# Prompt attention scores as three fp32r passes of split q and k, and a weight split moved behind the attention

## The chip, the cores and the metric

The kernel runs on one core of one Trainium2 chip. The metric is the device time of one execution in microseconds. A core has five engines that run side by side and meet at semaphores: TensorE (PE), VectorE (DVE), ScalarE (ACT), GpSimd (POOL) and SyncE (SP, which here issues DMAs).

## What is computed

One layer of a hybrid decoder: for 1,024 prompt tokens and 32 sample tokens (8 sequences of 4), with 1,024 channels. Each row is normalised and projected by one combined matrix; one half of the result goes through causal window sums, the other through an attention of 8 heads of 64 channels in which an indexer picks 256 admissible keys for each query. Then come an output projection with a residual add and an MLP with squared ReLU. The part that the change touches:

```python
def attend(q, kg, vg, valid):
    logits = jnp.einsum('bqhd,bqkhd->bqhk', q.astype(jnp.float32), kg.astype(jnp.float32)) * (HEAD_DIM ** -0.5)
    logits = jnp.where(valid[:, :, None, :], logits, NEG_INF)
    p = jax.nn.softmax(logits, axis=-1)
    out = jnp.einsum('bqhk,bqkhd->bqhd', p, vg.astype(jnp.float32))
...
h = x + jnp.einsum('bte,ed->btd', jnp.concatenate([pool_out, attn_out], axis=-1), w_out)
```

The kernel doesn't gather keys. It computes the scores of all keys up to the query's block, adds a mask that is 0 for picked keys and -1e30 for the others, and takes the softmax over the row.

## The kernel before

The program is written by hand, one instruction list for each engine, with semaphores between them. Numbers that need fp32 accuracy in cheap matmuls are **split**: `hi` is the value rounded to fp32r, `lo` the rest, and a product is the sum of three fp32r passes (`hi*hi`, `hi*lo`, `lo*hi`; the helper `three`). That holds for the input projection, the output projection and the MLP. The attention's own products (`qk`, the transposes `p_T`, the values `pv`) are plain fp32.

The stages in order: norm and input projection, with the indexer and a search for each query's threshold beside it; four small fp32 products of the window sums (`pooled` by `wpool`); the **prompt attention**; then sample attention mixed with the first output-projection tiles; the rest of the output projection; MLP up and down; final norm.

The prompt attention has 8 blocks of 128 queries (j = 0 to 7) and in each 4 units (c = 0 to 3) of two heads. A unit's scores have 128(j+1) columns, cut into halves of up to 512 (`n_half`). For unit u, PE does in this order: `p_T(2u)` (transposes of the first head's probabilities, L2262), `qk(u+2, (0,))` (first half of the scores of the unit after next), `p_T(2u+1)`, `qk(u+2, (1,))` (the second half, blocks 4 to 7 only), for every second unit `spread_T` (L2288), and `pv(u)`. In `qk` the two heads of a unit sit in rows 0 to 63 and 64 to 127 of `qT` and `kT`, and write to two PSUM banks:

```python
mm(ps[:, 0:w], qT[r0:r0 + DH, c, P * j:P * j + P],
   kT[r0:r0 + DH, c, 512 * hf:512 * hf + w], True, True).then_inc(fullof(name), 1)
```

DVE adds the mask and finds the row maximum (L1755), ACT takes the exponential (L1209), PE transposes, ACT and DVE copy the transposes to `probT` (L1017, L1789), and PE multiplies by the values. Beside that DVE prepares the mask of block j+3 in parts: `flag` and `eq` (L1718, L1720), a scan over ties (L1723), a compare and multiply of two SBUF tiles (L1725). POOL spreads the denominators (`spread`, L852), finishes masks (`mask_sum`, L867 and L870) and makes the low part of the attention output (`o_low`, L860), two `q` steps for each block, in the order of `rows_half`.

POOL also splits the weights. `proj_split(n)` (L690, L692) takes block n of the weight columns in four quarters, high and low part of each; only the last quarter's low part raises `s_wlo`, for which PE waits before it uses the block. Block n lies in slot n % 2 of `w_raw`, `w_hi` and `w_lo`. Blocks 0 to 18 belong to `w_in`; block 19, `N_OUT`, is the first of `w_out`. Before, `N_OUT` is split ahead of the attention:

```python
for n in range(5, N_OUT + 1):
    proj_split(n)
```

and `N_OUT + 1` and the next follow behind the last `o_low`. After the attention PE runs `page_T(0)` (transposes of a page of the sample's cache), then `k_tile(0)`, the first output tile: three transposes of the residual (L2403), the wait for `s_wlo`, and 24 fp32r products. SP issues its loads in one order; the load of weight block `N_OUT + 2` (L524) waits until block `N_OUT` is split, and the cache pages of the next units (L558) stand behind it.

## Time and profile before

| | us |
|---|---|
| median of 3 runs | 1364.81 |
| lowest and highest | 1363.1, 1366.77 |
| the profiled execution, its own time | 1369.43 |
| its span, first to last instruction | 1367.6 |
| mean granted TensorE clock | 0.985 |

The span is cut by the order of stages: the attention runs from about 315.7 to 449 us, the first output tile's fp32r products begin at 452.2. All times in rows are microseconds from the span's start unless marked ns. A matmul row's length reaches past the start of the next row, since matmuls are pipelined; what a product occupies is read from start to start. An fp32 product stands in the trace as two records. "64*128 64x512" is a product with 64 rows and 128 stationary columns, and 512 moving columns.

### The profile page before, as it was taken

What the parts mean: (1) busy time and instruction counts of PE and PEld (TensorE: products, weight loads), DVE (VectorE), ACT (ScalarE), POOL (GpSimd) and SP (SyncE); (2) the same over time, 40 slices, a digit from 0 to 9 for tenths busy, and PEclk for the clock granted to TensorE, in tenths of its full rate; (3) what the DMA queues carried; (4) which work ended last, traced back from release to release, by engine and by line L of the source; (5) the groups of instructions that cost most, each with busy time, mean ns of one, the idle gap of its engine ahead of it and who ended that gap; (6) DMA issues with size and microseconds to landing.
All of it is one profiled execution on the core that took longest, in us unless ns stands there. A gap on an engine that the chain in (4) does not pass through costs nothing.

```text
span 1367.6 us, 25243 instructions
## 1 busy us (share of the span) xinstructions
PE 1320.3 (97%) x9720; PEld 1222.1 (89%) x9720; DVE 696.3 (51%) x1611; ACT 533.6 (39%) x1075; POOL 583.8 (43%) x607
## 2 busy tenths in 40 slices
PE   5999999999999999999899999999899999999998
PEld 4958999995666899779899999999899999999997
DVE  6368996767985222237834434434534334333445
ACT  6344887737777222325433333333301110111034
POOL 5333984342330311321277667677233333333610
PEclk9999999998999999999999999999999999999999
DMA  6330113310000876772233323323521331232203
GB/s 196 84 90 16 47 55 95 94 48 1 1 25 25 280 230 197 250 237 93 79 110 126 106 84 126 110 79 126 190 94 63 110 110 64 92 110 103 68 2 127
DMA packets 143549, 141.68 MB, mean 104 GB/s; under 512 B 21080, under 2 KB 111320, under 8 KB 143423
## 3 DMA queue, kind: packets, MB, share of 16 engines
q1 hardware_dynamic: 124933, 116.31, 26.7%
q10 hardware_dynamic: 17842, 21.94, 4.4%
q0 software_dynamic: 656, 1.84, 0.6%
q8 instruction: 77, 1.26, 0.4%
q14 instruction: 41, 0.34, 0.1%
HBM read 111.87 MB, written 26.50 MB: 101 GB/s over the span
## 4 chain that ended last, share of the span: by engine, by line
PE 80%; DVE 7%; ACT 3%; issue 1%; POOL 0%; ACTq 0%; DVEq 0%; POOLq 0%
PE bank L2087 73%; PE bank L2262 3%; DVE junk L1664 3%; PE bank L2324 2%; ACT sjunk L1119 1%; DVE lack L1668 1%; PE bank L2403 1%; PE bank L2132 0%; PE bank L2591 0%; DVE cc_lo L1743 0%; DVE cand L1674 0%; DVE hid_lo L2012 0%; DVE sqacc L1875 0%; PE bank L2288 0%; DVE delta L1671 0%
## 5 line engine op out<-in xcount | busy, mean ns | idle before, releaser
L2087 PE MATMUL bank<-hid_hi,w_hi 128*128 128x384 f32 (+1 forms) x672 | 219.6, 327 | 3.9 <-DVE stg L1937 3.9
L2087 PE MATMUL bank<-hid_hi,w_lo 128*128 128x384 f32 (+1 forms) x672 | 218.0, 324 | 0.0
L2087 PE MATMUL bank<-hid_lo,w_hi 128*128 128x384 f32 (+1 forms) x672 | 215.4, 323 | 0.0
L2044 DVE TENSOR_TENSOR acc<-bank,acc 128x384 f32<-128x384 f32 x168 | 87.7, 524 | 206.6 <-PE bank L2087 206.6
L690 POOL TENSOR_TENSOR w_hi<-w_raw,zero 128x256 fp32r<-128x256 f32 x108 | 68.6, 635 | 207.1 <-PE bank L2087 190.6
L2087 PE MATMUL bank<-xn_hi,w_hi 128*128 128x384 f32 (+1 forms) x456 | 151.5, 332 | 2.0 <-POOL w_lo L692 1.3
L904 POOL TENSOR_TENSOR w_hi<-w_raw,zero 128x1024 fp32r<-128x1024 f32 x29 | 54.9, 1893 | 223.4 <-PE bank L2087 205.4
L2087 PE MATMUL bank<-xn_lo,w_hi 128*128 128x384 f32 (+1 forms) x456 | 148.1, 325 | 0.0
L2087 PE MATMUL bank<-xn_hi,w_lo 128*128 128x384 f32 (+1 forms) x456 | 147.6, 324 | 0.0
L1411 ACT ACTIVATE hid_hi<-hraw 128x1056 fp32r<-128x1056 f32 x32 | 32.7, 1077 | 258.2 <-PE bank L2087 167.2
L2087 PEld LDWEIGHTS bank<-hid_hi,w_hi 128*128 128x128 f32 x672 | 127.8, 190 | 4.2 <-DVE stg L1937 4.2
L2087 PEld LDWEIGHTS bank<-hid_hi,w_lo 128*128 128x128 f32 x672 | 127.6, 190 | 0.0
L2087 PE MATMUL bank<-hi_T,hn_hi 128*128 128x264 f32 x448 | 127.5, 285 | 0.0
L2087 PE MATMUL bank<-lo_T,hn_hi 128*128 128x264 f32 x448 | 127.0, 283 | 0.0
L2087 PE MATMUL bank<-hi_T,hn_lo 128*128 128x264 f32 x448 | 126.8, 283 | 0.0
L2087 PEld LDWEIGHTS bank<-hid_lo,w_hi 128*128 128x128 f32 x672 | 125.9, 188 | 0.0
L1119 ACT ACTIVATE sjunk<-score,cand 128x768 bf16<-128x768 f32 (+2 forms) x93 | 96.6, 1041 | 22.4 <-DVE cand L1674 18.0
L1664 DVE TENSOR_SCALAR_CACHE_REDUCE junk<-score,cand 128x384 uint8<-128x384 f32 (+1 forms) x124 | 101.7, 876 | 3.7
L2087 PE MATMUL bank<-hn_hi,hn_lo 128*128 128x264 f32 x336 | 95.7, 285 | 0.0
L2087 PE MATMUL bank<-hn_hi 128*128 128x264 f32 x336 | 95.5, 284 | 0.0
L2087 PE MATMUL bank<-hn_lo,hn_hi 128*128 128x264 f32 x336 | 95.2, 283 | 0.0
L908 POOL TENSOR_TENSOR w_lo<-w_raw,w_hi 128x1024 fp32r<-128x1024 f32 x32 | 77.2, 2414 | 38.0 <-ACT w_hi L1397 26.7
(300 smaller groups left out, 3227.2 us busy)
## 6 DMA issues: line engine op xcount, KB each, us to landing
w_raw<-in_w_ff_dram SPq DMA_DIRECT2D x50, 512.0 KB, 3.5
hraw<-hidden_dram SPq DMA_DIRECT2D x16, 1056.0 KB, 7.4
page<-in_cache_k_dram SPq DMA_DIRECT2D x64, 256.0 KB, 3.7
page<-in_cache_v_dram SPq DMA_DIRECT2D x64, 256.0 KB, 3.5
hidden_dram<-stg ACTq DMA_DIRECT2D x56, 264.0 KB, 2.0
w_raw<-in_w_in_dram SPq DMA_DIRECT2D x18, 512.0 KB, 3.6
wr<-in_w_ff_dram SPq DMA_DIRECT2D x14, 512.0 KB, 4.5
xrow<-in_x_prompt_dram SPq DMA_DIRECT2D x8, 512.0 KB, 8.1
```

What stands on the lines that cost most here:

```text
L690: nc.gpsimd.tensor_tensor(w_hi[n % 2][:, c], w_raw[n % 2][:, c], zero_w[:, 0:WP], ALU.add).then_inc(s_whi, 1)
L904: nc.gpsimd.tensor_tensor(w_hi[n[0] % 2][:, :], w_raw[n[0] % 2][:, :], zero_w, ALU.add).then_inc(s_whi, 1)
L908: nc.gpsimd.tensor_tensor(w_lo[n[0] % 2][:, :], w_raw[n[0] % 2][:, :], w_hi[n[0] % 2][:, :].bitcast(F), ALU.subtract).then_inc(s_wlo, 1)
L1119: nc.scalar.activation(sjunk[i % 2][0:r, 0:n], v, ACT.Sign, bias=cand[0:r, ND + i:ND + i + 1].bitcast(F), scale=-1.0, accum_out=cnt[0:r, N ...
L1411: nc.scalar.activation(hid_hi[slot][:, k, :], src[:, k, :], ACT.Copy).then_inc(s_hh, 1)
L1664: nc.vector.tensor_scalar(junk[0:r, i % 2, 0:n], v, cand[0:r, i:i + 1].bitcast(F), 0.0, ALU.is_lt, ALU.add, accum_out=cnt[0:r, i:i + 1]).t ...
L1668: nc.vector.tensor_tensor(lack[:, :], cnt[:, :], lim[:, :], ALU.is_gt).then_inc(s_bs, 1)
L2044: nc.vector.tensor_tensor(v, ps[:, 0:w], v, ALU.add).then_inc(freeof(("dn", gi, m, g)), 1)
L2087: return nc.tensor.matmul(out, lhsT, rhs, start=start, stop=stop)
L2262: last = nc.tensor.transpose(ps[:, P * (k - 4 * hf):P * (k - 4 * hf) + P], prob[:, i % 4, P * k:P * k + P], ident[:, :])
L2324: last = nc.tensor.transpose(ps[:, P * c:P * c + P], page[i % PS][:, j, P * c:P * c + P], ident[:, :])
L2403: nc.tensor.matmul(ps[:, P * (t - a):P * (t - a) + P], xblk[xi][:, t, :], ident[:, :], start=t == a, stop=False, is_transpose=True)
```

## The change

Four new tiles hold the split operands. `q_hi` and `q_lo` lie in the halves of the norm buffers that the attention output fills later, `k_lo` lies on `kT` itself, and `k_hi` lies on `w_hi` and `w_lo` of both slots. So no weight block can be split while the attention still reads `k_hi`: block `N_OUT` leaves the loop ahead of the attention and is split behind the last `o_low`, after a wait for the last scores. POOL splits q and k of blocks 0 and 1 before the attention and of block j+2 in the `spread` step of block j (`qk_split`, 4 instructions of 128x512, 8 calls). PE makes three passes for each pair of halves, both heads in turn within each pass, and waits for `s_qk` at the first unit of each block.

```diff
+        q_hi = at("q_hi", A_X + C4 * T * 4, [P, C4, T], R)
+        q_lo = at("q_lo", A_X + XN + C4 * T * 4, [P, C4, T], R)
+        k_hi = at("k_hi", A_W + 2 * KC * P * 4, [P, C4, NP], R)
+        k_lo = at("k_lo", A_K, [P, C4, T], R)
...
-            for n in range(5, N_OUT + 1):
+            for n in range(5, N_OUT):
                 proj_split(n)
...
+            def qk_split(j):
+
+                cols = slice(P * j, P * j + P)
+                zero_t = zero[:, 0:1].unsqueeze(2).broadcast_to([P, C4, P])
+                nc.gpsimd.tensor_tensor(k_hi[:, :, cols], kT[:, :, cols], zero_t, ALU.add).then_inc(s_qk, 1)
+                pool.wait_ge(s_qk, 4 * j + 1)
+                nc.gpsimd.tensor_tensor(k_lo[:, :, cols], kT[:, :, cols], k_hi[:, :, cols].bitcast(F), ALU.subtract).then_inc(s_qk, 1)
+                nc.gpsimd.tensor_tensor(q_hi[:, :, cols], qT[:, :, cols], zero_t, ALU.add).then_inc(s_qk, 1)
+                pool.wait_ge(s_qk, 4 * j + 3)
+                nc.gpsimd.tensor_tensor(q_lo[:, :, cols], qT[:, :, cols], q_hi[:, :, cols].bitcast(F), ALU.subtract).then_inc(s_qk, 1)
+
+            for c in range(C4):
+                for g in range(3):
+                    wait_evac(pool, ("proj", N_Q + c, g))
+            qk_split(0)
+            qk_split(1)
...
+                    if q % 2 == 0 and q // 2 + 2 < QB:
+                        qk_split(q // 2 + 2)
...
             o_low(2 * QB - 1)
-            for n in range(N_OUT + 1, N_OUT + KM + 2):
+            for u in (NU - 2, NU - 1):
+                for e in range(2):
+                    for hf in range(n_half(units[u][0])):
+                        wait_full(pool, ("qk", 2 * u + e, hf))
+            for n in range(N_OUT, N_OUT + KM + 2):
                 proj_split(n)
...
             def qk(u, halves=(0, 1)):
...
+                if c == 0 and halves[0] == 0:
+                    pe.wait_ge(s_qk, 4 * j + 4)
...
-                    for e in range(2):
-                        r0 = DH * e
-                        name = ("qk", 2 * u + e, hf)
-                        ps = begin(pe, name)
-                        mm(ps[:, 0:w], qT[r0:r0 + DH, c, P * j:P * j + P],
-                           kT[r0:r0 + DH, c, 512 * hf:512 * hf + w], True, True).then_inc(fullof(name), 1)
+                    for i, (a, b_) in enumerate(((q_hi, k_hi), (q_hi, k_lo), (q_lo, k_hi))):
+                        for e in range(2):
+                            r = slice(DH * e, DH * e + DH)
+                            name = ("qk", 2 * u + e, hf)
+                            ps = bank[plan[name][0]] if i else begin(pe, name)
+                            last = mm(ps[:, 0:w], a[r, c, P * j:P * j + P], b_[r, c, 512 * hf:512 * hf + w], i == 0, i == 2)
+                            if i == 2:
+                                last.then_inc(fullof(name), 1)
```

On POOL ahead of the attention, the instructions between the last `w_in` block and the first `spread`; before:

```order
L690 TENSOR_TENSOR w_hi_138<-w_raw_136,zero 128x256 [waits bank5_full,weights_loaded1]
L692 TENSOR_TENSOR w_lo_140<-w_raw_136,w_hi_138 128x256 [waits weights_high]
...
L852 COPY rdenb<-rden 128x256 [waits denominator] x2
L867 TENSOR_TENSOR cum<-cum,flag 128x512 [waits mask_ties_ranked]
L870 TENSOR_SCALAR score<-cum 128x512 [waits mask_summed]
```

and with the change:

```order
L866 TENSOR_TENSOR k_hi<-kT,zero 128x4x128 [waits bank3_free,bank4_free,bank2_free,bank5_free,bank1_free,bank0_free]
L868 TENSOR_TENSOR k_lo<-kT,k_hi 128x4x128 [waits attention_operands_split]
L869 TENSOR_TENSOR q_hi<-qT,zero 128x4x128
L871 TENSOR_TENSOR q_lo<-qT,q_hi 128x4x128 [waits attention_operands_split]
...
L859 COPY rdenb<-rden 128x256 [waits denominator]
L866 TENSOR_TENSOR k_hi<-kT,zero 128x4x128
L868 TENSOR_TENSOR k_lo<-kT,k_hi 128x4x128 [waits attention_operands_split]
L869 TENSOR_TENSOR q_hi<-qT,zero 128x4x128
L871 TENSOR_TENSOR q_lo<-qT,q_hi 128x4x128 [waits attention_operands_split]
L859 COPY rdenb<-rden 128x256 [waits denominator]
```

The eight instructions of weight block `N_OUT` are gone from here; blocks 0 and 1 of k and q stand in their place, and block 2 stands between the first and the second `spread`.

On POOL behind the attention, before:

```order
L860 TENSOR_TENSOR cc_lo<-onorm,cc_hi 128x2x128 [waits attention_high]
L852 COPY rdenb<-rden 128x256 [waits bank7_full,denominator]
L860 TENSOR_TENSOR cc_lo<-onorm,cc_hi 128x2x128 [waits attention_high] x2
L690 TENSOR_TENSOR w_hi_137<-w_raw_135,zero 128x256 [waits bank2_full,weights_loaded0]
L692 TENSOR_TENSOR w_lo_139<-w_raw_135,w_hi_137 128x256 [waits weights_high]
```

and with the change:

```order
L884 TENSOR_TENSOR cc_lo<-onorm,cc_hi 128x2x128 [waits attention_high]
L859 COPY rdenb<-rden 128x256 [waits bank7_full,denominator]
L884 TENSOR_TENSOR cc_lo<-onorm,cc_hi 128x2x128 [waits attention_high] x2
L697 TENSOR_TENSOR w_hi_142<-w_raw_140,zero 128x256 [waits bank2_full,bank1_full,bank0_full,bank3_full,weights_loaded1,bank5_full]
L699 TENSOR_TENSOR w_lo_144<-w_raw_140,w_hi_142 128x256 [waits weights_high]
```

The first split behind the last `o_low` was that of slot 0 (block `N_OUT + 1`) and is now that of slot 1 (block `N_OUT`), with slot 0 behind it. On PE the reader of that block has not moved:

```order
L2437 MATMUL bank<-ident,xblk_68 128x128 [waits x_block0,bank6_free,attention_low]
L2437 MATMUL bank<-ident,xblk_68 128x128 x2
L2117 MATMUL bank<-cc_hi,w_hi_142 128x384 [waits weights_low]
L2117 MATMUL bank<-cc_lo,w_hi_142 128x384
L2117 MATMUL bank<-cc_hi,w_lo_144 128x384
```

It is still the first output tile, directly behind the three residual transposes, and `w_hi_142` is slot 1.

## Rows read from the trace of the kernel before

**Rows 1.** The page: engines over the span, then the chain by engine.

```profile
PE 1320.3 (97%) x9720; PEld 1222.1 (89%) x9720; DVE 696.3 (51%) x1611; ACT 533.6 (39%) x1075; POOL 583.8 (43%) x607
...
PE 80%; DVE 7%; ACT 3%; issue 1%; POOL 0%; ACTq 0%; DVEq 0%; POOLq 0%
```

**Rows 2.** Stretches of the attention: length, busy time of each engine, PEclk, DMA.

```profile
316.00:334.40 18.40, 16.73 (x86) 9.20 (x83) 13.57 (x63) 11.39 (x45) 4.28 (x7) 0.63 0.00 1
334.40:361.00 26.60, 26.60 (x226) 16.64 (x224) 25.16 (x80) 22.24 (x64) 9.12 (x13) 1.00 0.01 2
361.00:376.70 15.70, 15.02 (x123) 9.42 (x123) 14.10 (x48) 11.24 (x27) 5.04 (x6) 1.00 0.01 2
376.70:400.70 24.00, 23.64 (x211) 15.36 (x211) 20.66 (x66) 16.48 (x40) 7.93 (x15) 1.00 0.01 2
400.70:436.50 35.80, 35.80 (x317) 23.00 (x316) 22.20 (x76) 25.39 (x50) 6.73 (x9) 1.00 0.11 30
```

**Rows 3.** Chain of waits between 361 and 376.7 us, shares of that stretch.

```profile
by line: PE bank L2087 24.2%; DVE prob L1755 20.7%; DVE cum L1723 11.9%; issue 11.4%; PE bank L2262 9.6%; DVE flag L1718 8.1%; DVE nmx L1774 4.6%; DVE eq L1720 3.1%; DVE probT L1789 2.5%; DVE rden L1797 1.1%; DVE need L1722 0.9%; DVE mx L17
```

**Rows 4.** Timeline of PE in block 6: start, length, engine, line, operation, operands.

```profile
403.99 1.13 PE L2087 MATMUL bank<-kT,qT 64*128 64x512 f32 x4
405.05 0.98 PE L2262 MATMUL bank<-ident,prob 128*128 128x128 f32 x7
405.96 0.92 PE L2087 MATMUL bank<-kT,qT 64*128 64x384 f32 x4
```

**Rows 5.** PE's timeline, score products of 128 columns.

```profile
366.21 0.49 PE L2087 MATMUL bank<-kT,qT 64*128 64x128 f32 x4
366.63 0.44 PE L2288 MATMUL bank<-ident,rdenb 128*128 128x128 f32 x2
```

**Rows 6.** PE's timeline, fp32 products over 128 rows, 4,224 columns in all.

```profile
308.49 7.26 PE L2087 MATMUL bank<-pooled,wpool 128*128 128x384 f32 x24
```

**Rows 7.** The chain in order of time: fp32r products, 288 and 384 columns.

```profile
207.49 3.20 PE bank L2087 x24
210.79 4.21 PE bank L2087 x24
```

**Rows 8.** Timeline of DVE, one scan; of DVE and POOL, sums beside a split.

```profile
373.67 2.71 DVE L1723 TENSOR_TENSOR_SCAN cum<-eq 128x1024 f32<-128x1024 bf16 x1
...
602.69 1.22 DVE L1875 TENSOR_TENSOR sqacc<-sqacc,sqt 128x384 f32<-128x384 f32 x2 [5.76 <-ACT sqt L1309]
606.36 1.89 POOL L904 TENSOR_TENSOR w_hi<-w_raw,zero 128x1024 fp32r<-128x1024 f32 x1 [12.03 <-PE bank L2087]
607.00 4.08 DVE L1875 TENSOR_TENSOR sqacc<-sqacc,sqt 128x256 f32<-128x256 f32 x2 [3.09 <-ACT sqt L1309]
```

**Rows 9.** One line on POOL: minimum/median/maximum ns, first and last start.

```profile
L933 POOL TENSOR_TENSOR hn_lo<-w_raw,hn_hi x49: 1289/1297/1310, 683.7 to 941.3; 128x512 fp32r<-128x512 f32 x49
```

**Rows 10.** Timeline of ACT and POOL at the attention's start.

```profile
308.69 0.41 ACT L1017 ACTIVATE qT<-bank 128x288 f32<-128x288 f32 x1 [2.71 <-PE bank L2087]
...
321.56 0.40 POOL L852 COPY rdenb<-rden 128x256 f32<-128x256 f32 x1 [17.81 <-DVE rden L1797]
```

**Rows 11.** Timeline of POOL after the attention, first and last of eight.

```profile
451.69 0.61 POOL L690 TENSOR_TENSOR w_hi<-w_raw,zero 128x256 fp32r<-128x256 f32 x1
...
456.52 0.73 POOL L692 TENSOR_TENSOR w_lo<-w_raw,w_hi 128x256 fp32r<-128x256 f32 x1
```

**Rows 12.** PE's timeline, first product that reads w_out.

```profile
452.20 0.42 PE L2087 MATMUL bank<-cc_hi,w_hi 128*128 128x384 f32 x1
```

**Rows 13.** PE's timeline, an earlier wait for a split.

```profile
662.17 0.69 PE L2087 MATMUL bank<-hn_hi,w_hi 128*128 128x384 f32 x1 [5.53 <-POOL w_lo L908]
```

**Rows 14.** Stretches after two waits of PE, columns as in rows 2.

```profile
662.20:665.40 3.20, 3.20 (x10) 3.20 (x11) 3.20 (x2) 1.16 (x2) 2.71 (x1) 0.50 0.13 46
...
976.90:982.90 6.00, 6.00 (x20) 6.00 (x21) 0.23 (x1) 4.25 (x5) 2.10 (x1) 0.50 0.97 367
```

**Rows 15.** Timeline of SP's issues after the attention.

```profile
452.86 0.42 SPq L524 DMA_DIRECT2D w_raw<-in_w_out_dram  x1
```

More of the change, by code:

```diff
@@ L195, in hymba_pool_dsa_step @@
         assert C4 * NB * HQ + G * SK <= moff[QB] and C4 * NB * HQ + G * (SK + (NPG + 1) * P) <= moff[QB] + T
+        q_hi = at("q_hi", A_X + C4 * T * 4, [P, C4, T], R)
+        q_lo = at("q_lo", A_X + XN + C4 * T * 4, [P, C4, T], R)
+        k_hi = at("k_hi", A_W + 2 * KC * P * 4, [P, C4, NP], R)
+        k_lo = at("k_lo", A_K, [P, C4, T], R)
+        assert C4 * NP <= 4 * KC * P
         acc = at("acc", A_Q, [P, KC, T], F)
@@ L460, in hymba_pool_dsa_step @@
         s_rd = sem("denominator")
+        s_qk = sem("attention_operands_split")
         s_exp_on = sem("exponential_loaded")
```

## The prediction

> **What bounds the kernel now.** I read the page first: PE is busy for 97% of the span and makes up 80% of the chain that ended last [rows 1], so a change counts by what it does to PE's path. The second view cuts the attention into stretches [rows 2]. PE is busy nearly throughout, but so is DVE in some: 25.2 of 26.6 us from 334.4 to 361, 14.1 of 15.7 up to 376.7, 20.7 of 24 up to 400.7. Only from 400.7 on has DVE much room (22.2 of 35.8). In the first stretch the granted clock is 0.63 on average, so most of it ran at 1.2 GHz and not 2.4. The third view, the chain between 361 and 376.7 us, gives PE's matmul line only 24% and DVE's lines over half [rows 3]: there a faster score product doesn't help. Then the timeline of PE shows what a score product occupies, and the timelines around 452 us show who needs the moved weight block.
>
> **What the score products cost.** A pair of halves (two heads) starts at 403.99 and PE's next work at 405.05: 1.06 us for 512 columns [rows 4]. For 128 columns it is 366.21 to 366.63, 0.42 us [rows 5]. A line through both gives 1.67 ns a column and 0.21 us fixed; so 0.85 for 384 and 0.63 for 256 columns. Full-height fp32 products, 4,224 columns in 7.26 us, take 1.72 ns a column for one product [rows 6]. A pair costs as much as one, so the two heads run side by side in their row halves.
>
> An fp32r pass takes 3.20/24 = 0.133 us for 288 columns and 4.21/24 = 0.175 for 384 [rows 7], a line that gives 0.232 for 512, 0.119 for 256 and 0.063 for 128. No row shows an fp32r pair in row halves. If it runs side by side as the fp32 pairs do, a pair costs 0.21 plus three passes: 0.90, 0.73, 0.57 and 0.40 us for 512, 384, 256 and 128 columns. If it doesn't, it costs 0.21 plus six: 1.60, 1.26, 0.92 and 0.59. I take the first, since the nearest rows (same operand places, same banks) show it. There are 24 pairs of 512 columns and 8 of each other width. **Gross gain:** 24 x 0.16 + 8 x (0.12 + 0.06 + 0.02) = 5.4 us; at the lower clock the four pairs of block 1 save about twice as much, 0.3 more: 5.7. The other end is a loss of 24 x 0.54 + 8 x (0.41 + 0.29 + 0.17) = 19.9.
>
> A rule speaks of the same quantity. The Trainium skill's page FP8 and Floating Point Precision (section Matmul Precision) says that true fp32 is four passes through the array; by its count three in place of four would take a quarter off. Of the 40.6 us that all pairs take that is 10.2, and the sum below would end 4.8 us lower. The rows disagree in size: a pass of fp32r has 0.45 ns a column against 0.42 in fp32, and the fixed 0.21 us isn't divided.
>
> **How much of 5.7 reaches the end.** By stretch [rows 2]: up to 334.4 blocks 0 and 1 can save 0.6, and I take 0.5. Up to 361 blocks 2 and 3 can save 1.1, but DVE has 1.4 us of room, which the next part eats; 0.3. Up to 376.7 nothing [rows 3]. Up to 400.7 about 1.2, of which 0.8; up to 436.5 about 2.1, of which 1.5, because the second half's product also covers the copies of the transposed probabilities, and in every second unit nothing else stands between. That makes 3.1.
>
> **The new POOL work.** A subtraction of 128x512 on POOL takes 1.30 us [rows 9]; the add with zero is bounded by 0.61 (half as wide) [rows 11] and that 1.30, and I take 1.1. One `qk_split` is 2 x (1.1 + 1.3) = 4.8 us (3.8 to 5.2). The last q columns leave ACT at 309.1, so block 0 is split by 313.9; PE ends the window products at 315.7 [rows 6, 10], so `qk(0)` doesn't wait. Block 1 is done by 318.7, ahead of the first `spread` at 321.56 [rows 10]. That cover is 1.8 us; if it fails, PE waits for the rest. The later splits stand in POOL's queue before an `o_low` and the next `spread`, half a block (4 us and more) later; I cost the queue at nothing. Where POOL is late, the second `spread` of block 0 is the first to show it.
>
> But POOL's instruction holds up DVE's with two SBUF operands. Two sums of 384 columns took 1.22 us together; two of 256 beside a weight split took 4.08 [rows 8]. The six later splits fall on DVE's scans (2.71 us the largest) and some of its multiplies [rows 8], with a delay between nothing and one POOL instruction each: 0 to 1.3 us, six to nine times. Up to 361 this is in my 0.3; for the rest I take 0.6 off. **Net gain of the attention: 2.5 us**, with ends at 5.7 and at -1. The Trainium skill says the same of the cause (GPSIMD Engine Reference, Specifications: the SBUF interfaces are shared with VectorE, contention with two SBUF inputs), and the trace agrees. By that rule every scan beside a split would wait, which would put the gain nearer 1.
>
> **The moved weight split.** Ahead of the attention its removal gives nothing: POOL idles 17.8 us there anyway [rows 10]. Behind it, POOL's first split of a block runs from 451.69 to 457.25, eight instructions [rows 11], and there is now block `N_OUT`. PE reads it at 452.20 [rows 12] and gets `s_wlo` only at the end: **5.1 us** of wait, with nothing else for PE since its queue is in order. The last `o_low`, which starts the split, ends with the attention, so this wait doesn't shrink when the attention does. Block `N_OUT+1` is then done at 462.8, long before the fourth output tile. SP holds the load at 452.86 [rows 15] and the pages behind it until 457.3, 4.4 us; PE itself is 5.1 later, so I cost that at nothing.
>
> Such a wait also costs clock. A wait of 5.53 us for a split [rows 13] was followed by work at 0.50 until 665.4, 3.2 us; after another wait, of 3.9 us, 6.0 us of work ran at 0.50 [rows 14]. Half of it is lost: 1.6 to 3.0 us. I take **2.3**.
>
> **Sum:** -2.5 + 5.1 + 2.3 = +4.9 us on the profiled execution's 1369.4, so 1374.3. That execution lies 4.6 us above the median of 1364.8; for the median I say **1369.7**. A measurement of this kernel can tell about 0.3%, 4.1 us, from no change.
>
> **Rivals.**
> *The gain arrives whole.* PE's savings are not eaten by DVE: -5.7 + 5.1 + 1.6 to 3.0 gives +1 to +2.4, near 1366.5. For it: PE leads the chain in four of five stretches. Against: DVE at 95% between 334 and 361. By the page's count of passes it would be -2.8, 1362. Together 0.27.
> *The clock returns earlier in the attention* (faster). From 316 to 334.4 the mean is 0.63, about 13.6 us at half speed [rows 2], worth up to 6.8 us of PE time. The change alters how PE is loaded there. If all of it went and the gain came whole: 1.7 - 6.8 = -5.1, 1359.7. It decides when over 5.8 of the 6.8 come back; DVE, 13.6 of 18.4 busy, makes that unlikely. Chance 0.05.
> *More half-speed work or DVE in the lead.* A further 3.4 us at 0.50 within the attention costs 1.7, and all scans held up bring the gain to 0: +9, 1373.9. Chance 0.12.
> *The fp32r pair isn't side by side*: +19.9 + 7.4 = +27, 1392. Against it, only the fp32 rows. Chance 0.04.
> *The change doesn't do what it says* would be `qk(0)` held by a late split; past its 1.8 us of cover each us costs one. That is inside the range.
>
> **How the numbers follow.** The forecast has 0.52, the others 0.27, 0.05, 0.12 and 0.04. Of the forecast's share about 0.4 lies above +4.1, with the two slower rivals 0.56 to 0.6; the 0.27 and the rest of the forecast are no measurable change. So faster 0.05, same 0.37, slower 0.58. The range takes in the first and third rivals: 1364.5 to 1374.5.
>
> **What would show it.** Right: the pairs' start-to-start falls to about 0.90 and 0.73 us; an idle of about 5 us before the first fp32r product of `w_out`, released by POOL, then some us at clock 0.50; scans longer than before beside the new splits; the attention 2 to 3 us shorter. Wrong: pairs of 1.6 us; no idle at that place; or an attention shorter by 5 us or more.

## The result, and the profile after

The changed kernel took 1374.88 us (median of 4 runs, 1374.75 to 1375.19), the kernel before 1364.70 (4 runs, 1363.1 to 1366.77). The ratio is 1.0074, with a 95% interval of 1.0057 to 1.0091: slower by 10.2 us, where +4.9 was forecast and 1374.5 was the upper end of the range. The profiled execution took 1374.97 us with a span of 1373.2. Against the profiled execution of before (1369.43, span 1367.6) that is +5.5, which is nearly the forecast. The two comparisons don't agree, since the profiled execution of before lies above all four of those runs; the section on the reasons comes back to that.

The page after, engines and chain (compare [rows 1]):

```profile
PE 1317.8 (96%) x9816; PEld 1231.7 (90%) x9816; DVE 698.4 (51%) x1611; ACT 533.7 (39%) x1075; POOL 630.5 (46%) x639
...
PE 76%; DVE 9%; ACT 3%; issue 2%; POOL 1%; DVEq 0%; ACTq 0%; POOLq 0%
```

POOL has 32 more instructions and 46.7 us more of work; PE is busy for 2.5 us less. PE's share of the chain fell by 4 points, and DVE, issue and POOL took them.

PE's timeline in block 6 (compare [rows 4]):

```profile
405.03 0.50 PE L2117 MATMUL bank<-k_hi,q_hi 64*128 64x512 f32 x2
405.37 0.40 PE L2117 MATMUL bank<-k_lo,q_hi 64*128 64x512 f32 x2
405.60 0.39 PE L2117 MATMUL bank<-k_hi,q_lo 64*128 64x512 f32 x2
405.92 0.98 PE L2296 MATMUL bank<-ident,prob 128*128 128x128 f32 x7
406.84 0.45 PE L2117 MATMUL bank<-k_hi,q_hi 64*128 64x384 f32 x2
407.12 0.34 PE L2117 MATMUL bank<-k_lo,q_hi 64*128 64x384 f32 x2
407.30 0.34 PE L2117 MATMUL bank<-k_hi,q_lo 64*128 64x384 f32 x2
407.57 0.44 PE L2322 MATMUL bank<-ident,rdenb 128*128 128x128 f32 x2
```

A pair of 512 columns takes 0.89 us from its start to the next work (405.03 to 405.92), one of 384 takes 0.73. Each row holds the two instructions of one pass, one for each head. The three rows of a pair start 0.34 and 0.23 us apart, where one product of 512 columns over all rows would take 0.23 by the line through [rows 7], and six of them 1.39. So the fp32r products of two heads do run side by side in their row halves.

The stretches of the attention (compare [rows 2]):

```profile
334.40:361.00 26.60, 25.39 (x242) 18.14 (x240) 24.99 (x70) 22.31 (x64) 23.74 (x21) 0.99 0.01 2
361.00:376.70 15.70, 14.36 (x134) 10.19 (x136) 14.16 (x52) 10.03 (x26) 10.30 (x11) 1.00 0.01 2
376.70:400.70 24.00, 22.38 (x230) 16.57 (x228) 20.89 (x67) 17.42 (x40) 18.34 (x22) 1.00 0.00 1
400.70:436.50 35.80, 35.51 (x361) 26.77 (x361) 23.83 (x79) 26.04 (x53) 6.98 (x9) 1.00 0.10 31
```

Where POOL went from 9 to 24 us (first row) and from 8 to 18 (third), PE's busy time fell by 1.2 and 1.3 us, and PE stands idle instead. Between 355 and 366 us the chain of waits changes its leader. The first line is from before, the second from after:

```profile
by line: PE bank L2087 68.7%; PE bank L2262 29.3%; PE bank L2288 3.3%
```

```profile
by line: DVE prob L1785 37.3%; issue 30.7%; DVE cum L1755 12.0%; DVE flag L1748 8.4%; DVE eq L1750 5.5%; PE bank L2117 4.5%; DVE cum L1753 3.4%; DVE nmx L1804 2.5%; DVE nmx L1807 1.7%; DVE rden L1827 1.6%; DVE mx L1785 1.1%; DVE onorm L1836
```

The timelines of POOL and DVE there show what happened:

```profile
356.14 0.40 POOL L859 COPY rdenb<-rden 128x256 f32<-128x256 f32 x1 [1.21 <-DVE rden L1827]
356.50 1.04 POOL L866 TENSOR_TENSOR k_hi<-kT,zero 128x512 fp32r<-128x512 f32 x1
357.62 1.28 POOL L868 TENSOR_TENSOR k_lo<-kT,k_hi 128x512 fp32r<-128x512 f32 x1
358.85 2.76 POOL L869 TENSOR_TENSOR q_hi<-qT,zero 128x512 fp32r<-128x512 f32 x1
361.69 1.28 POOL L871 TENSOR_TENSOR q_lo<-qT,q_hi 128x512 fp32r<-128x512 f32 x1
```

```profile
357.68 3.10 DVE L1753 TENSOR_TENSOR_SCAN cum<-eq 128x896 f32<-128x896 bf16 x1
```

In before the same scan, of 896 columns, took 2.01 us:

```profile
357.45 2.01 DVE L1723 TENSOR_TENSOR_SCAN cum<-eq 128x896 f32<-128x896 bf16 x1
```

The scan comes to its turn 0.06 us after `k_lo` started, stands until 358.85, and then takes its 2.0. `q_hi` stands until the scan is through and takes the rest of its own 1.0 after that. The later of the two stands until the earlier is through: DVE is 1.1 us later, POOL 1.7. The Trainium skill has this as a rule (SBUF — State Buffer, section "SBUF: two separate sides": an exclusive lock, whichever starts first has it for the whole instruction), and the trace agrees.

POOL paid this at every split beside the attention: the two splits ahead of it take 4.74 us each, the six others 5.9 to 6.8, of which the four from 343 us on 6.5 to 6.8. DVE paid at some: of the six scans, three are longer than in before (two by 0.5 to 0.6 us, one by 1.1) and three are not. One of those three had stood behind POOL already in before, where an `o_low` was under way when it came to its turn:

```profile
373.51 0.73 POOL L860 TENSOR_TENSOR cc_lo<-onorm,cc_hi 128x256 fp32r<-128x256 f32 x1 [1.61 <-ACT cc_hi L1225]
```

So the 2.71 us of [rows 8] hold a wait. In the kernel with high parts by copy (below) the scan of 1,024 columns met almost none:

```profile
373.02 2.29 DVE L1755 TENSOR_TENSOR_SCAN cum<-eq 128x1024 f32<-128x1024 bf16 x1
```

POOL's queue was the second thing. Half a block earlier a split had made the next `spread` late, and PE waited for it:

```profile
351.20 0.39 POOL L859 COPY rdenb<-rden 128x256 f32<-128x256 f32 x1
```

```profile
351.64 0.44 PE L2322 MATMUL bank<-ident,rdenb 128*128 128x128 f32 x2 [0.86 <-POOL rdenb L859]
```

Its input `rden` was ready at 349.51, while the split was still running. In [rows 10] the first `spread` had followed its `rden` at once.

Last, the moved weight split: the wait of PE, and the stretches of the wait, of the work at half clock behind it, and of the work after (compare [rows 12, 14]):

```profile
456.57 0.69 PE L2117 MATMUL bank<-cc_hi,w_hi 128*128 128x384 f32 x1 [4.83 <-POOL w_lo L699]
```

```profile
451.76:456.57 4.81, 0.00 (x0) 0.00 (x0) 0.39 (x1) 0.00 (x0) 4.58 (x8) 0.76 0.44 122
456.57:461.14 4.57, 4.57 (x14) 4.57 (x15) 0.00 (x0) 0.00 (x0) 4.33 (x7) 0.50 0.76 257
461.14:470.00 8.86, 8.86 (x84) 8.33 (x84) 1.38 (x2) 1.63 (x3) 0.83 (x2) 1.00 1.00 323
```

PE stands for 4.8 us, the granted clock falls within that wait, and PE then works at 1.2 GHz for 4.57 us, of which half is lost: 2.3.

### The profile page after: what moved, and what is told of

It is laid out like the page before. It is cut to its first block, busy times and chain, and to the rows that moved or that the text cites. A ratio compares the mean times of both kernels' runs of the same rounds, so it can differ in the third digit from the quotient of the medians.

```text
span 1373.2 us, 25484 instructions
## 1 busy us (share of the span) xinstructions
PE 1317.8 (96%) x9816; PEld 1231.7 (90%) x9816; DVE 698.4 (51%) x1611; ACT 533.7 (39%) x1075; POOL 630.5 (46%) x639
## 4 chain that ended last, share of the span: by engine, by line
PE 76%; DVE 9%; ACT 3%; issue 2%; POOL 1%; DVEq 0%; ACTq 0%; POOLq 0%
PE bank L2117 70%; DVE junk L1694 3%; PE bank L2358 2%; PE bank L2296 2%; ACT sjunk L1149 1%; DVE prob L1785 1%; DVE lack L1698 1%; PE bank L2437 1%; PE bank L2162 0%; PE bank L2625 0%; DVE cc_lo L1773 0%; DVE cand L1704 0%; DVE hid_lo L2042 0%; DVE sqacc L1905 0%; DVE delta L1701 0%
```

## The experiments

Two measures need explaining. The first: the attention has 16 reciprocals `rden`, one for each half block q, and they mark its course. The time from the sixth to the last (q=5 to q=15) lies behind the half-clock work of the attention's start and ahead of the wait for the weight block, so it compares the attention's inside at full clock, in all kernels but the one with the splits at odd q. In before it was 97.12 us in both profiles of that kernel, and in after 96.93 and 96.84 in its two.

The second runs from the last of these reciprocals to the next one, in the sample attention, and holds the wait for the weight block with the clock behind it. From 446.96 to 553.66 in before it is 106.70 us, in after 113.83 and in its second profile 113.99:

```profile
446.96 0.17 DVE L1797 RECIPROCAL rden<-den 128x4 f32<-128x4 f32 x1
553.66 0.15 DVE L1856 RECIPROCAL rden<-den 128x1 f32<-128x1 f32 x1
```

```profile
446.27 0.17 DVE L1827 RECIPROCAL rden<-den 128x4 f32<-128x4 f32 x1
560.10 0.15 DVE L1886 RECIPROCAL rden<-den 128x1 f32<-128x1 f32 x1
```

So the moved split costs 7.1 to 7.3 us there.

**The kernel before, profiled again.** No edit.

> The kernel before, unchanged, profiled once more. Its runs spread from 1363.1 to 1366.8 us and its profiled execution took 1369.4, while those of the changed kernel lie within 0.5 us and its profiled execution among them. Theory: executions of the kernel before differ by stretches of work at a granted clock of 0.50 after waits of PE (each costs about 1.7 us per 3.4 us of stretch), and the profiled one had more of them than the median one. Then a new profile near 1365 shows less half-clock time than the first one, by about 2 x 4.5 = 9 us in all. Rival: the profiled execution was longer in idle time (transfers, semaphores) at the same clock; then the half-clock stretches are the same and idle gaps of PE are longer.

It came out at 1365.73 us (10 runs, 1360.71 to 1369.78), ratio to the kernel before 0.9995 (0.998 to 1.0011). The profiled run was again the longest: 1369.78 at a mean granted clock of 0.985, with the same stretches at half clock as in the first profile, but for one of 3.4 us that lies at 28 us and not at 106. So the place of the difference within an execution was not seen. What was seen is the list of runs. Over these 10 and the 68 runs of before that stand beside the experiments, the fastest took 1360.5 us at a mean clock of 0.995 and the slowest 1371.7 at 0.984, and on the whole the mean time falls as the clock rises (1367.8 at 0.987, 1366.3 at 0.989, 1363.7 at 0.993). (1 - clock) times the span is 6.8 us in the fastest and 21.9 in the slowest, 15 apart where the times are 11 apart. The list supports the theory. Since both profiles are of long executions, it doesn't rule out that waits differ as well.

**The move alone.** The kernel before with

```
-            for n in range(5, N_OUT + 1):
+            for n in range(5, N_OUT):
...
-            for n in range(N_OUT + 1, N_OUT + KM + 2):
+            for n in range(N_OUT, N_OUT + KM + 2):
```

> The kernel before with only the weight split of block N_OUT moved behind the last o_low; scores stay fp32, no splits of q and k. Theory A (the loss is the moved split): PE waits about 5 us before its first w_out product of block N_OUT and then works some 7 us at half clock, so +6.5 us or more (4.4 to 5.1 of wait, 2.3 of clock), +8 to +10 if a later stretch of half clock comes on top, since the changed kernel is 10.2 above the median. Theory B (the loss sits in the new work of POOL inside the attention): +4 us or less here.

1372.26 us against 1365.90, ratio 1.0052 (1.0033 to 1.0071): +6.4. PE's wait is the same 4.83 us as in after, and the work behind it runs at half clock. q=5 to q=15 took 96.89 us, and from the last reciprocal to the next 113.52, 6.8 more than in before. Theory A gets its lower number. The move is about two thirds of the loss, and not the 8 to 10 us which would have made it all.

**Splits that nobody reads.** The changed kernel, its score products replaced by those of before:

```
-                    for i, (a, b_) in enumerate(((q_hi, k_hi), (q_hi, k_lo), (q_lo, k_hi))):
...
+                    for e in range(2):
...
+                        mm(ps[:, 0:w], qT[r0:r0 + DH, c, P * j:P * j + P],
+                           kT[r0:r0 + DH, c, 512 * hf:512 * hf + w], True, True).then_inc(fullof(name), 1)
```

> The changed kernel with all its splits of q and k on POOL and PE's wait for them, but the score products are the fp32 ones of the kernel before (the parts are made and not read; the low part of k goes to the place of the low part of q, so that k stays whole). Against the kernel with the move alone it prices POOL's new work. Theory A (queue and port cost little): 0 to 1 us above the move alone. Theory B (POOL's splits hold DVE's scans and the spreads, and eat the gain of the products): 2 to 5 us above the move alone. Against the changed kernel it prices the products: 5 to 6 us above it if the products gain their whole worth, 1 to 2 if DVE and POOL hide them anyway.

1376.68 us, 4.4 above the move alone (ratio to before 1.0086, 1.0064 to 1.0107). q=5 to q=15 took 99.08, 2.2 more than with the move alone. The scan of 896 columns took 3.08 us here too:

```profile
358.02 3.08 DVE L1753 TENSOR_TENSOR_SCAN cum<-eq 128x896 f32<-128x896 bf16 x1
```

So POOL's new work costs 2.2 us in that part, and 4.4 in the whole of a run. Of the rest the profiles show 0.7 from q=0 to q=5 (27.99 against 27.29) and 1.0 from the last reciprocal to the next (114.49 against 113.52), but there the stretches at half clock differ too. Against the kernel that does use the splits, the products gain 2.2 us from q=5 to q=15 (99.08 to 96.9). The medians give 2.2 as well (1376.7 to 1374.5 of the repeat below), but the runs of the two kernels overlap. Theory B holds in size for the splits, theory A's "5 to 6 us" for the products doesn't.

**The weight split in a gap.** In POOL's program, after:

```
-            rows_half(QB + 2, 2 * QB)
-            o_low(2 * QB - 1)
+            rows_half(QB + 2, 2 * QB - 1)
...
-            for n in range(N_OUT, N_OUT + KM + 2):
+            proj_split(N_OUT)
+            rows_half(2 * QB - 1, 2 * QB)
+            o_low(2 * QB - 1)
+            for n in range(N_OUT + 1, N_OUT + KM + 2):
```

> The changed kernel, but the weight split of block N_OUT runs on POOL between the o_low of q=13 and the spread of q=15, as soon as the last scores are read, and not behind the last o_low. Theory A (the loss of the change is that wait with its clock): the wait before the first w_out product goes, and the time falls by 5 us of wait and 2 to 5 of clock: 1365 to 1368. What is left against the kernel before is then the net of products and POOL work, about -0.7 by the attention's end in the traces. Theory B: the split delays the last spread and o_low instead, and the gain is under 3 us.

1367.53 us, ratio to before 1.0018 (1.0005 to 1.003). POOL's timeline, first and last of the split, then the last spread:

```profile
437.49 0.61 POOL L697 TENSOR_TENSOR w_hi<-w_raw,zero 128x256 fp32r<-128x256 f32 x1
...
442.32 0.73 POOL L699 TENSOR_TENSOR w_lo<-w_raw,w_hi 128x256 fp32r<-128x256 f32 x1
445.47 0.40 POOL L859 COPY rdenb<-rden 128x256 f32<-128x256 f32 x1 [2.42 <-DVE rden L1829]
```

The split ends 2.4 us ahead of the next `spread`, and PE goes into the first `w_out` product without a wait and at full clock. From the last reciprocal to the next it is 106.70 us, as in before. 7 us of the loss were the place of that one block, and this place was allowed: the last scores are read by then, so nobody needs `k_hi` any more. 1.6 us are left. q=5 to q=15 takes 96.95, as in before, and the mean clock of the runs was 0.988 against 0.9895; what the 1.6 us are made of isn't shown.

**The splits at odd q.** On top of the kernel with the split in the gap:

```
-                    if q % 2 == 0 and q // 2 + 2 < QB:
-                        qk_split(q // 2 + 2)
                     if q >= 1:
                         o_low(q - 1)
+                    if q == 0:
+                        qk_split(2)
+                    if q % 2 == 1 and q // 2 + 3 < QB:
+                        qk_split(q // 2 + 3)
```

> The kernel with the split of block N_OUT in the gap, and the splits of q and k moved in POOL's order: block 2 behind o_low at q=0, blocks 3 to 7 behind o_low at odd q, where DVE runs no scan; before, they stood behind the spread at even q, beside the scans. In the traces so far the half blocks from q=5 to q=15 take 96.89 us with the move alone, 99.08 with the unused splits and 96.95 with splits and products; 1.97 of those 2.2 us come in q=6 and q=7, where a scan went from 2.01 to 3.08 us and a spread waited behind a split. Theory B (splits beside scans and before the spread are the price): scans return to 2.01 and 2.71 us, q=5 to q=15 falls to about 95 us, and the time to 1365.5. Rival C (POOL's work itself is the price, wherever it stands): the spread or o_low that now waits is another one, and q=5 to q=15 stays at 97.

A miss of 7 us: 1372.65, ratio to before 1.0058 (1.0036 to 1.008). At odd q POOL has its mask sums to do and the next `spread` comes soon. Two of the splits met a scan there too (at 332 and 359 us) and took 5.9 and 6.7 us; the three others at odd q took 4.8 to 5.0. The next `spread` stood behind the whole split:

```profile
359.28 2.86 POOL L871 TENSOR_TENSOR q_lo<-qT,q_hi 128x512 fp32r<-128x512 f32 x1
362.09 0.39 POOL L859 COPY rdenb<-rden 128x256 f32<-128x256 f32 x1
```

```profile
362.54 0.33 PE L2326 MATMUL bank<-ident,rdenb 128*128 128x128 f32 x1 [3.09 <-POOL rdenb L859]
```

Two such waits, 3.29 us at 335.8 and 3.09 at 362.5, both followed by half clock, stand against the 5 us lost to the kernel with the split in the gap. q=5 to q=15 took 99.08, but here this part holds one of the waits and the half clock behind it (3.4 us from 363.2). Without these 3.1 and 1.7 us it would be some 94.3, an estimate, as short as with no later splits at all (below). Theory B was half of the matter: the scan of that block took 2.32 us in place of 3.09, where it had said 2.01, and the queue cost more than the lock had.

**High parts by copy.** On top of the split in the gap, for `k_hi`, and for `q_hi` alike:

```
-  nc.gpsimd.tensor_tensor(k_hi[:, :, cols], kT[:, :, cols], zero_t, ALU.add)
+  nc.gpsimd.tensor_copy(k_hi[:, :, cols], kT[:, :, cols])
```

> The kernel with the split of block N_OUT in the gap, and the high parts of q and k made by POOL's copy (one operand) in place of the add with zero. Theory (only an instruction with two operands in SBUF shuts DVE's out, and the other way round): a q_hi beside the scan takes its undisturbed time in place of 2.2 to 3.0 us, the low parts still hold DVE, the copy takes 0.6 to 1.04 us, and q=5 to q=15 falls by 0.5 to 1 us, the time to 1366.5 to 1367. Rival: a copy is held by DVE like the add, and nothing changes.

1365.82 us, ratio to before 0.9998 (0.9983 to 1.0014). q=5 to q=15 falls to 94.76.

```profile
355.10 0.62 POOL L866 CAST k_hi<-kT 128x512 fp32r<-128x512 f32 x1
355.80 1.28 POOL L868 TENSOR_TENSOR k_lo<-kT,k_hi 128x512 fp32r<-128x512 f32 x1
357.02 2.35 POOL L869 CAST q_hi<-qT 128x512 fp32r<-128x512 f32 x1
359.45 1.28 POOL L871 TENSOR_TENSOR q_lo<-qT,q_hi 128x512 fp32r<-128x512 f32 x1
```

A copy alone takes 0.62 us where the add with zero took 1.04, so a split is 0.84 us shorter. But the copy beside the scan took 2.35: it waited for the scan as the add had. The reason given in the expectation is wrong, since with one operand too POOL waited for the scan, and the gain from q=5 to q=15 is 2.2 us where 0.5 to 1 was expected. POOL's instructions are the whole edit, so they are the cause: a split beside the attention takes 5.0 to 5.9 us in place of 5.9 to 6.8. Which of the waits behind them went first wasn't taken apart.

**The wait filled.** The changed kernel, in PE's first `w_out` tile, before its wait for the low parts:

```
+                    if m == 0 and g == 0:
+                        fill = begin(pe, ("proj", n, 1))
+                        for _i in range(28):
+                            mm(fill[:, 0:384], cc_hi[:, C4, 0:P], cc_hi[:, C4, 0:384], True, True)
                     pe.wait_ge(s_wlo, n + 1)
```

> The changed kernel, with PE's wait of 4.8 us before the first w_out product filled by 28 fp32r products of 384 columns into the bank of the next tile, which that tile's first transposes overwrite; nothing else is altered and no result is. 28 x 0.16 = 4.5 us and a start-up, so the wait nearly goes from idle to busy and the first real product starts when it did, at most 0.5 us later. Theory (the idle costs clock on top of its own length): no stretch of granted clock 0.50 follows at 454 us, and the time is 2 to 3 us below the changed kernel. Rival (the half-clock stretch comes from something else, or costs nothing because other engines lead there): the stretch or the time stays, 0 to 0.5 us.

1371.45 us (7 runs, 1370.28 to 1373.07) against 1374.5 for the changed kernel again (below). The first stretch is the filled wait, the second the work behind it:

```profile
451.00:456.00 5.00, 5.00 (x29) 4.68 (x29) 0.21 (x1) 0.00 (x0) 4.76 (x8) 1.00 0.39 114
456.00:461.10 5.10, 5.10 (x34) 5.06 (x33) 0.01 (x1) 0.88 (x2) 4.79 (x8) 1.00 0.87 271
```

The first real product starts 5.65 us after POOL's first split instruction, 5.58 in after, so the wait is as long as it was; only PE was busy in it. The clock stays at 1.00. From the last reciprocal to the next it is 111.84 us: 5.1 more than in before, which is the wait, and 2.0 to 2.2 less than in the two profiles of after, which is the clock's share, with nothing else changed. The medians are 3.05 us apart, with runs that overlap; what they show above those 2.0 to 2.2 isn't placed.

**The changed kernel again.** No edit.

> The changed kernel once more, unchanged, for comparison with the variants on the same chip. Its first four runs lay within 0.5 us at 1375, at a granted clock of 0.985; runs of the kernel before spread over 9 us, from 1360.7 at 0.995 to 1369.8 at 0.985. Theory (executions differ only by how many half-clock stretches they draw, 3.4 us each and 1.7 us of loss): over more runs the changed kernel spreads too, its median falls below 1375 and the difference to the kernel before shrinks towards 8 us. Rival: it always pays all of its stretches, and stays at 1375.

1374.5 us (6 runs, 1371.96 to 1376.6) against 1365.47, ratio 1.0072 (1.0049 to 1.0094). It does spread, so its first four runs were close together by chance. But its median hardly falls, and the difference is 9 to 10 us, not 8. Its mean clock was 0.986. The profiled run had 0.991 and a span of 1370.2, 3.0 less than the first profile: the stretches of half clock at 106 and 201 us are absent from it, and the one at the attention's start is 3.4 us in place of 13.7. The wait of 4.82 us and the half clock behind it are there as in the first.

The two profiles show one thing more. From q=0 to q=5 they took 28.00 and 27.99 us, each step between two reciprocals the same to 0.01 us, though 13.7 us ran at half clock in the one and 3.4 in the other. So at the attention's start half clock cost the changed kernel nothing, since something other than PE's products set the pace. The fp32 kernels took 28.52 us there with 13.7 us at half clock (both profiles of before) and 27.29 with 8.6 (the move alone).

**The products alone.** On top of the split in the gap: no splits of q and k for blocks 2 to 7, whose products read other data of the same shape.

```
-                    if q % 2 == 0 and q // 2 + 2 < QB:
-                        qk_split(q // 2 + 2)
...
+                    ops = ((q_hi, k_hi), (q_hi, k_lo), (q_lo, k_hi)) if j < 2 else ((cc_hi, cc_hi),) * 3
```

> The kernel with the split of block N_OUT in the gap, without the splits of q and k for blocks 2 to 7: PE makes the same number of fp32r products of the same shapes there, on other data (the attention of these blocks is not the reference's). It gives the products' gain with none of POOL's work beside it. The half blocks from q=5 to q=15 took 96.89 us with fp32 products and no splits, 99.08 with splits alone, 96.95 with both. Theory B: POOL's later splits cost 2.2 us there whatever the products are, so 94.7 us here and about 1365.0 in time. Rival (the products' gain is itself hidden behind DVE, and the splits cost only where PE isn't ahead): 95.5 to 96.5 us, and the time stays within 1 us of the kernel with the splits.

q=5 to q=15 took 94.17 us: 2.7 less than with fp32 products, 2.8 less than with the splits beside them. The median is 1363.97, ratio to before 0.9992 (0.9981 to 1.0003): even without the later splits the products don't make the whole clearly faster. Theory B again. In that part of the attention the table of four is complete:

| q=5 to q=15 | no later splits | with them |
|---|---|---|
| fp32 products | 96.89 | 99.08 |
| three passes | 94.17 | 96.95 |

**Three blocks ahead.** High parts by copy, both copies ahead of both subtractions, `qk_split(0)` to `(2)` ahead of the attention and `qk_split(q // 2 + 3)` at even q.

> The kernel with high parts by copy, with three blocks split ahead of the attention in place of two (blocks 3 to 7 at q=0, 2, 4, 6, 8) and both copies ahead of both subtractions. A split takes 3.8 us now, so three end near 320.6, where the first spread is due at 320.4. Theory: one split fewer beside DVE's scans and the first subtraction later than the scan's start; q=0 to q=15 took 123.7 us and falls by 1 to 2, the time to 1364 to 1365. Rival: a subtraction that waits for a scan still ends late and holds the spread behind it, as with the splits at odd q, where PE waited 3.3 and 3.1 us for a spread; then it is no faster or slower by 1 to 3.

1364.33 us, ratio to before 0.9994 (0.9985 to 1.0003). q=0 to q=15 is 122.8 us, 0.9 less than with two blocks ahead (123.7). The direction is the theory's, but against the kernel before it can't be told from no change.

**All copies, and their control.** The last kernel with the high parts of POOL's weight splits made by `tensor_copy` as well, and the kernel before with that edit alone (three lines of the form `nc.gpsimd.tensor_copy(w_hi[n % 2][:, c], w_raw[n % 2][:, c])`).

> As the kernel with three blocks split ahead, and the high parts of all weight blocks that POOL splits made by its copy too (0.61 in place of 1.04 us for 512 columns). The weight splits also stand before waits of PE: 5.5 to 5.9 us at 652 to 664 and 3.9 at 970 to 980. Theory (these waits are POOL's two passes over a block, and the first pass is 2.1 of some 4.8 us): each wait shortens by 1 to 2 us, the time falls by 2 to 4 below the kernel with three blocks ahead, 1360 to 1362, faster than the kernel before. Rival: the transfer of the block or ACT's part leads there, and nothing changes.

> The kernel before with the same edit of the weight splits alone, as the control: if it falls as much as the theory gives the kernel with all copies (2 to 4 us, to 1362 or 1363), that gain has nothing to do with the scores, and the difference between the two is what the fp32r scores are worth after all: 1 to 2 us by the attention's length so far (123.7 against 125.6). Rival: no change, 1365.5.

1359.39 us, ratio 0.9954 (0.9939 to 0.9969), and 1359.65, ratio 0.9959 (0.9944 to 0.9974). Both beat both kernels, and they can't be told apart: the gain is that of the copies, and the fp32r scores add nothing that the whole shows. From q=5 to q=15 they are 2.3 us shorter (94.66 against 96.95), but the mean clock of these runs was 0.989 and that of the control 0.992; whether that takes the 2.3 us back isn't shown. The gain didn't come from where the theory had it. The waits at 650 and 965 us are still 5.8 and 3.9. What has gone is a wait of 1.9 us ahead of the attention, with the half-clock work behind it. In before, PE's timeline and the stretches:

```profile
200.67 0.63 PE L2132 MATMUL bank<-ident,vchunk 128*128 128x128 f32 x4 [1.92 <-ACT vrow L1017]
```

```profile
198.75:200.67 1.92, 0.00 (x1) 0.03 (x1) 1.89 (x5) 1.92 (x7) 1.84 (x4) 1.00 0.00 0
200.67:204.70 4.03, 4.03 (x16) 4.03 (x17) 3.84 (x8) 2.52 (x5) 3.87 (x5) 0.58 0.48 130
```

In the control PE has no wait there, and the clock stays at 1.00:

```profile
196.00:206.00 10.00, 10.00 (x68) 9.90 (x67) 7.72 (x16) 8.07 (x15) 7.34 (x9) 1.00 0.20 54
```

That wait ended with ACT, whose copies out of PSUM stand between its steps of the search for each query's threshold. DVE's part of that search has an addition of 7 columns that reads two SBUF tiles, once in each of 31 steps. Before, then the control (minimum, median and maximum in ns):

```profile
L1674 DVE TENSOR_TENSOR cand<-cand,delta x31: 166/167/2373, 126.2 to 286.4; 128x7 int32<-128x7 int32 x31
```

```profile
L1674 DVE TENSOR_TENSOR cand<-cand,delta x31: 165/167/583, 124.2 to 280.9; 128x7 int32<-128x7 int32 x31
```

Its longest wait beside POOL's splits went from 2.4 to 0.6 us, and the 31 steps take 3.5 us less. That speaks for POOL's shorter instructions holding DVE less. It accounts for 3.5 us of the 6; how much of the rest is the missing wait's clock and how much differs between executions anyway wasn't taken apart.

## Why the prediction was right and wrong

**The price of a pair** was right to 0.01 us: 0.90 and 0.73 forecast, 0.89 and 0.73 measured. A pair of 512 columns became 16% shorter. That the halves run side by side was a choice from the fp32 rows, and it held.

**The gain of the products** was right too. From 361 us on the forecast had 0, 0.8 and 1.5 in its last three stretches, 2.3 together; the experiment without the later splits gives 2.7 from q=5 (350 us) on.

**"The later splits stand in POOL's queue ... I cost the queue at nothing", and "for the rest I take 0.6 off"**: this is the step that failed within the attention. The splits cost 2.2 us (fp32 products) to 2.8 (three passes) from q=5 to q=15, not 0.6. Two things were missed. The lock works both ways: I let POOL hold DVE, by up to one instruction, and didn't let DVE's scan hold POOL, which made a 4.7 us split one of 5.9 to 6.8. And "half a block (4 us and more) later" isn't enough room for 6.5 us when an `o_low`, a `spread` and two mask sums want the same queue. Net, the attention became 0.7 us shorter between the two profiles (POOL's first weight split 451.69 before [rows 11], 450.99 after) where I had 2.5. The sentence that the rule of the shared interfaces "would put the gain nearer 1" was the better number, but by luck: it let every scan wait for POOL, and in the trace three of six became longer while POOL waited at all six.

**The moved split** was right: 5.1 us of wait forecast, 4.83 measured; 2.3 us of clock forecast, 2.3 read off the trace, and 2.0 to 2.2 gained by filling the wait. The pieces on the profiled executions make -0.7 + 4.8 + 2.3 = +6.4, and 0.5 more has come by 785 us, of which 0.3 lies in a wait of 5.85 us in place of 5.53 [rows 13]. Of that, the half clock behind the wait at 980 us gives back 1.5: 3.0 us of work in after, 6.0 in before [rows 14]. Measured +5.5, forecast +4.9. That the two are so near is in part luck: the attention gave 1.8 us less than forecast, and the shorter half clock at 980 us, which was not forecast, made up for most of it.

**"That execution lies 4.6 us above the median ...; for the median I say 1369.7"** is the step that cost the range. It carries an offset of 4.6 us over from one kernel to the other; for the changed kernel it was 0.1 (1374.97 against 1374.88). The profiled execution of before has a mean clock of 0.985, where its runs have 0.9895 on average; the changed kernel has about as little in most runs, 0.9847 in the first four and 0.986 in the repeat. So the forecast held for two executions that are alike in clock, and not for the medians.

(1 - clock) times the span is 14.4 us for the usual execution of before and 19 to 21 for the changed kernel, of which the one wait explains 3.4 (half clock for 6.8 us). But this product is no price of its own. At the attention's start the changed kernel takes 28.0 us with much half clock or little. The fp32 kernels take 28.5 with much and 27.3 with less. The profiled execution of before had much, so against it such a loss doesn't show: up to 1.2 us of the 4.6 by these two numbers. The rest of the 4.6 isn't placed.

From the medians of the runs: the move +6.4, POOL's splits +4.4, the products -2.2, in sum +8.6, where the two sets of runs of the changed kernel give +9.0 and +10.2. The last term was read as a difference to the repeat, so the sum comes near by construction and tests nothing.

**Rivals.** The gain didn't arrive whole, the pairs ran side by side, `qk(0)` wasn't late. The third rival, more half-speed work and DVE in the lead (+9, chance 0.12), is nearest to what happened, though the profile of after has no further stretch of half clock within the attention. I gave it too little, since the row that spoke for it, DVE busy for 25.2 of 26.6 us [rows 2], was at hand.

What stays open: why kernels with the splits draw more half-clock work outside of the one wait. The kernel with the split in the gap has no such wait and still has a mean of 0.988 against 0.9895, 2 us by the same product, and its median is 1.6 us above before's. No run changes the clock alone there, and the spread of the mean clock over the runs of one kernel is larger than this difference.

## What to carry to other kernels

When a change gives POOL work beside DVE, price both queues in both directions: the sum of the two instructions, and then who stands behind the later one. When a change moves an operand's preparation to after the last use of its room, look for a place in the queue before the reader that still meets that condition; here it was one half block earlier and worth 7 us. And if single executions spread with the clock, forecast the difference between kernels from like executions, and don't let one execution's distance to its median stand for another kernel's.

## What the runs showed of the hardware

- POOL's copy from fp32 to fp32r takes 0.62 us for 128x512 where the add with zero takes 1.04, and 0.40 against 0.61 for 128x256. Used for POOL's weight splits in the kernel before, it gave 6 us over the whole kernel (ratio 0.9959, 0.9944 to 0.9974).
- POOL's one-operand copy waits for a DVE scan like a two-operand add: 2.35 us beside the scan, 0.62 alone. The Trainium skill's GPSIMD Engine Reference (section Specifications) puts the condition of two SBUF inputs on DVE's instruction, and the trace agrees: the scan reads `eq` as both of its inputs.
- From q=5 to q=15 two executions of one kernel agree to 0.1 us (97.12 twice; 96.93 and 96.84), though the second two are 3.0 us apart in span. All runs of the kernel before lie up to 11 us apart, with a mean granted clock from 0.984 to 0.995.
- Keeping PE busy with products that nobody reads, during a wait of 4.8 us, held the granted clock at 1.00 and gave 2.0 to 2.2 us in the part that holds the wait (3.05 between the medians).
- Half clock doesn't cost everywhere: at the attention's start, from q=0 to q=5, the changed kernel took 28.00 us with 13.7 us at half clock and 27.99 with 3.4.
